# One stage in place of combining, residual, last norm and store, and an earlier split of the last expert's lower weights

## The reference

```python
def expert_block(args):
    idx, w, e = args
    xb = tok_pad[idx]
    hb = jax.nn.silu(xb @ ex_gate[e]) * (xb @ ex_up[e])
    return (hb @ ex_down[e]) * w[:, None]
...
ffn = _hier_moe(_modulate(x, sh2, sc2), ...)
x = _layernorm(ALPHA * x + g2 * ffn, ln2_g[l], ln2_b[l])
```

## Time and profile before

| | us |
|---|---|
| median of three runs | 3562.02 |
| the profiled execution, its own time | 3566.95 |
| span of the profiled execution | 3565.2 |
| from the last expert's result copy (DVE, 3486.77) to the end of the span | 78.4 |
| PE busy, share of the span | 88% |
| DVE busy, share of the span | 56% |
| mean granted TensorE clock | 0.946 |

### The profile page before, as it was taken

One profiled execution on the slowest core, in us unless ns is written; L12 is line 12 of the kernel. 1 busy time (PEld: TensorE's weight loads), 2 busy tenths in 40 slices (PEclk: granted clock), 3 DMA queues, 4 the chain that ended last, 5 costly groups with the idle time before them and its releaser, 6 DMA issues. The chain is left out here.

```text
span 3565.2 us, 53470 instructions
## 1 busy us (share of the span) xinstructions
PE 3146.9 (88%) x21844; PEld 2464.7 (69%) x21844; DVE 2002.8 (56%) x2748; ACT 1284.8 (36%) x1613; POOL 910.2 (26%) x472
## 2 busy tenths in 40 slices
PE   7968999997999978999889998389997869999993
PEld 5446887796777756887678766268885358888882
DVE  3756551301433346553399447775644359998983
ACT  2543322222333333332232212312222247777772
POOL 3013443342222213443312300010100014454530
PEclk9989999999999989999999998699998979999996
DMA  3631222321111111222311100401001149999992
GB/s 137 235 119 71 94 94 83 124 95 71 60 60 60 60 48 71 94 94 84 106 48 60 59 17 1 176 23 50 26 26 75 47 168 360 364 372 367 374 355 100
DMA packets 76463, 439.37 MB, mean 123 GB/s; under 512 B 14832, under 2 KB 17904, under 8 KB 27376
## 3 DMA queue, kind: packets, MB, share of 16 engines
q1 hardware_dynamic: 66768, 427.12, 32.3%
q0 software_dynamic: 9504, 9.47, 0.8%
HBM read 421.85 MB, written 39.85 MB: 130 GB/s over the span
## 5 line engine op out<-in xcount | busy, mean ns | idle before, releaser
L76 POOL TENSOR_TENSOR ring_lo<-ring,unit_hi 128x2048 fp32r<-128x2048 f32 x116 | 536.2, 4624 | 1206.3 <-ACT unit_hi L71 1206.3
L122 PE MATMUL wide<-h_hi,unit_hi 128*128 128x512 f32 x1296 | 519.7, 401 | 99.9 <-DVE h_lo L182 43.5
L124 PE MATMUL wide<-h_hi,ring_lo 128*128 128x512 f32 x1296 | 519.1, 401 | 0.0
L123 PE MATMUL wide<-h_lo,unit_hi 128*128 128x512 f32 x1296 | 518.0, 400 | 0.0
L3013 DVE TENSOR_TENSOR ex_w_lo<-ring,ex_w_hi 128x2048 fp32r<-128x2048 f32 x192 | 437.2, 2287 | 43.5 <-ACT ex_w_hi L2966 41.6
L2966 ACT CAST ex_w_hi<-ring 128x2048 fp32r<-128x2048 f32 x192 | 365.7, 1908 | 103.7 <-DMA ring<-in_weights 91.1
L71 ACT CAST unit_hi<-ring 128x2048 fp32r<-128x2048 f32 x116 | 220.3, 1900 | 459.3 <-PE wide L124 450.7
L122 PEld LDWEIGHTS wide<-h_hi,unit_hi 128*128 128x128 f32 x1296 | 250.9, 194 | 178.6 <-POOL ring_lo L76 70.7
L123 PEld LDWEIGHTS wide<-h_lo,unit_hi 128*128 128x128 f32 x1296 | 247.0, 191 | 53.2 <-issue 0.2
L124 PEld LDWEIGHTS wide<-h_hi,ring_lo 128*128 128x128 f32 x1296 | 246.4, 190 | 52.7
L363 DVE TENSOR_TENSOR ffn_hidden_lo<-ffn_whole,ffn_hidden_hi 128x512 f32 (+1 forms) x44 | 201.5, 4579 | 50.6 <-ACT ffn_hidden_hi L338 50.6
(11 more groups left out here) (528 smaller groups left out, 6205.2 us busy)
## 6 DMA issues: line engine op xcount, KB each, us to landing
ring<-in_weights SPq DMA_DIRECT2D x356, 1024.0 KB
factors<-rp_out SPq DMA_DIRECT2D x8, 1536.0 KB, 5.5
rw_F<-factors SPq DMA_DIRECT2D x12, 1024.0 KB, 5.6
cb_both<-pair_rows_out SPq DMA_DIRECT2D x4, 1024.0 KB, 4.8
x<-in_x SPq DMA_DIRECT2D x1, 2048.0 KB, 7.5
x_kept<-x SPq DMA_DIRECT2D x1, 2048.0 KB, 12.2
x<-x_kept SPq DMA_DIRECT2D x1, 2048.0 KB, 8.9
x_mixing<-x SPq DMA_DIRECT2D x1, 2048.0 KB, 10.7
```

What stands on the lines that cost most here:

```text
L76: pool.tensor_tensor(self.lo[n % RING][:, :], self.ring[n % RING][:, :], self.hi[n % 2][:, :].bitcast(F32), ALU.subtract).then_inc(lo_read ...
L122: pe.matmul(dst, a[0], b[0], start=start, stop=False)
L123: pe.matmul(dst, a[0], b[1], start=False, stop=False)
L124: return pe.matmul(dst, a[1], b[0], start=False, stop=stop)
```

## The change

Two edits. The last expert's two down units are split in step 31, right after its gating product, and no longer at the start of step 32. And the four blocks after the experts become one, `tail_stage`: SP issues all four loads at once, each with a semaphore of its own; ACT scales `x` by ALPHA meanwhile; PE transposes each chunk of features into a PSUM bank of its own; DVE adds gate times that bank to `x` straight from PSUM; PE sums each chunk as it is added; the norm is the class `Norm`, with two buffers for the squares; and each of the 8 chunks is stored (256 KiB each) as soon as it is placed.

```diff
                 def step(e, j2, s):
-                    if s >= 1:
+                    if 1 <= s < EXPERTS:
                         for n in range(2):
                             hi(e, down_at(s - 1, n))
...
                         hi(e, gate_up_at(s + 1, 2))
+                    elif s == EXPERTS - 1:
+                        for n in range(2):
+                            hi(e, down_at(s, n))
...
-                    if s >= 1:
+                    if 1 <= s < EXPERTS:
                         for n in range(2):
                             lo(e, down_at(s - 1, n))
...
                         lo(e, gate_up_at(s + 1, 2))
+                    elif s == EXPERTS - 1:
+                        for n in range(2):
+                            lo(e, down_at(s, n))
...
-def combine_stage(nc, c, route, pair_rows, y):
+def tail_stage(nc, c, route, pair_rows, x, gate, scale, shift, out):
...
+        both, squares, rstd = sb("both", [P, TT, 2, D]), sb("squares", [P, 2, T]), sb("rstd", [P, T])
+        norm = Norm(c, x, x, x, scale, shift, c.bank[0], c.bank[1], squares, rstd[:, :])
...
                 for t in range(TT):
                     sp.dma_start(both[:, t, :, :].rearrange("p n d -> p (n d)"),
-                                 pair_rows[2 * P * t:2 * P * (t + 1), :].rearrange("(p n) d -> p (n d)", n=2)).then_inc(loaded, 16)
-
-                    sp.wait_ge(loaded, 16 * (t + 1))
+                                 pair_rows[2 * P * t:2 * P * (t + 1), :].rearrange("(p n) d -> p (n d)", n=2)).then_inc(loaded[t], 16)
+                for k in range(DC):
+                    sp.wait_ge(norm.placed, k + 1)
+                    sp.dma_start(out[:, k, :], x[:, k, :]).then_inc(stored, 16)
+                sp.wait_ge(stored, 16 * DC)
+
+            @block.scalar
+            def _(act):
+                for m in range(DC):
+                    act.mul(x[:, m, :], x[:, m, :], ALPHA).then_inc(grown, 1)
+                norm.scalar(act)
 
             @block.vector
             def _(dve):
                 for t in range(TT):
-                    dve.wait_ge(loaded, 16 * (t + 1))
+                    dve.wait_ge(loaded[t], 16)
...
-                for t in range(TT):
-                    dve.wait_ge(turned, 2 * t + 2)
-                    dve.tensor_copy(y[:, 4:8, t * P:(t + 1) * P], c.wide[t][:, T:D].rearrange("p (k t) -> p k t", k=4)).then_inc(high_done, 1)
+                for k in range(DC):
+                    dve.wait_ge(turned, k + 1)
+                    dve.wait_ge(grown, k + 1)
+                    dve.scalar_tensor_tensor(out=x[:, k, :], in0=c.bank[k], scalar=gate(k), in1=x[:, k, :], op0=ALU.mult,
+                                             op1=ALU.add).then_inc(added, 1)
+                norm.vector(dve)
 
             @block.tensor
             def _(pe):
                 for t in range(TT):
                     pe.wait_ge(summed, t + 1)
                     for k in range(DC):
-                        mm = pe.transpose(c.wide[t][:, k * P:(k + 1) * P], both[:, t, 0, k * P:(k + 1) * P], c.ident[:, :])
-                        if k % 4 == 3:
+                        mm = pe.transpose(c.bank[k][:, t * P:(t + 1) * P], both[:, t, 0, k * P:(k + 1) * P], c.ident[:, :])
+                        if t == TT - 1:
                             mm.then_inc(turned, 1)
...
+                for k in range(DC):
+                    pe.wait_ge(added, k + 1)
+                    norm.sum_chunk(pe, k)
+                pe.wait_ge(added, 2)
+                norm.sum_squares(pe)
...
-        combine_stage(nc, c, route, pair_rows, dev)
-        last_residual_stage(nc, c, x, dev, at(5))
-        layer_norm_stage(nc, c, x, x, T, col("ln2_g"), col("ln2_b"), "ln2")
...
+        tail_stage(nc, c, route, pair_rows, x, at(5), col("ln2_g"), col("ln2_b"), out)
```

More of the change, by code:

```diff
@@ L3053, in experts_stage, with sb @@
     w.at += ALL
-def combine_stage(nc, c, route, pair_rows, y):
+def tail_stage(nc, c, route, pair_rows, x, gate, scale, shift, out):
     with ExitStack() as ctx:
-        both = ctx.enter_context(nc.sbuf_tensor("cb_both", [P, TT, 2, D], F32))
-        loaded, scaled, summed, turned, low_done, high_done = c.semaphores("cb", ("loaded", "scaled", "summed", "turned", "low_done", "high_done"))
+        def sb(n, shape):
+            return ctx.enter_context(nc.sbuf_tensor(f"tail_{n}", shape, F32))
+        both, squares, rstd = sb("both", [P, TT, 2, D]), sb("squares", [P, 2, T]), sb("rstd", [P, T])
+        norm = Norm(c, x, x, x, scale, shift, c.bank[0], c.bank[1], squares, rstd[:, :])
+        fresh = norm.use(c.semaphores("tail", [f"norm_{n}" for n in Norm.NAMES] + [f"loaded{t}" for t in range(TT)] + [
+            "grown", "scaled", "summed", "turned", "added", "stored"]))
+        loaded, (grown, scaled, summed, turned, added, stored) = fresh[:TT], fresh[TT:]
         with nc.Block() as block:
```

## The result

The changed kernel takes 3543.15 us (median of 6 runs, 3533.86 to 3546.82) against 3567.41 us before (6 runs, 3556.59 to 3572.75): 24.3 us between the medians, a ratio of 0.9928 with a 95% interval of 0.9914 to 0.9941 (21 to 31 us). 27.0 had been forecast, for 3535.0 us. Of the 8.2 us between 3535.0 and 3543.15, 5.4 are the base (the median of before rose from 3562.02 to 3567.41 with three more runs) and 2.7 the gain. The profiled execution of after took 3534.85 us (span 3533.1), that of before 3566.95.

A forecast was written before the change was run, and what follows sets the result against it. PE, busy 88% of the span, bounds most of the kernel; gains lie in the last 100 us. Terms 6.2 + 6.35 + 8.6 + 1.85 + 4.0 = 27.0 us, off 3562.0, give 3535.0 us, range 3525 to 3547.

The forecast's parts named there:

- C: Last load's landing to end of sums over x: 13.0 us instead of 21.6, saving 8.6 us (7.4 to 11.5).
- E: Eight stores at the end: span ends 2.9 us after the last chunk instead of 6.87, saving 4.0 us.
- A: Earlier split before the last down product: 3.2 us less waiting and 3.0 from the kept clock, saving 6.2 us.
- Rival 1: Clock lost after shorter gaps and transposes don't start its rise: 5.3 us less, saving 21.7, 3540.3 us; chance 0.14.
- B: Four tail loads issued at once: last lands 12.9 us after first issue instead of 19.25, saving 6.35 us.
- rival 2: Four tail loads finish together near 12.9 us: 6.2 us less, saving 20.8, 3541.2 us; chance 0.09.
- D: Norm after the sums over x: 20.40 us instead of 22.25, with PE's clock kept, saving 1.85 us.
- Rival 3: Last expert's split comes no earlier because unit 191 lands after 3473: saving 20.8, 3541.2 us; chance 0.05.
- Rival 5: Changed step code makes the experts' loop stall PE each pass: at 1.5 us costs 46.5, giving 3581.5 us; chance 0.03.

The follow-up runs named there:

- e1: Kernel before with only the earlier split of the last two down units, the blocks after the experts unchanged; 3.6 us faster than before (0.9991).
- e5: Changed kernel with the late split and five idle float32 matmuls on PE in the gap before the last down product; 24.7 us under before.
- e6: Changed kernel with PE waiting for all four sums before its first transpose, so 32 run in one piece; 19.8 us faster than before (0.9946).
- e8: Changed kernel with early loads plus idle PE matmuls before the last down product and in the tail; 28.3 us faster than before (0.9924).
- e2: Changed kernel with the split of the last two units put back to the start of step 32; 23.4 us faster than before (0.9938).
- e0: Changed kernel run again without an edit, on the chip of other runs; 26.6 us faster than before (0.9930).
- e7_early_loads: Changed kernel with SP issuing the four loads within the experts' block once the last scatters landed; 28.5 us under before (0.9922).
- e3: Changed kernel with SP waiting for each of the four loads before issuing the next; 15.8 us faster than before (0.9953).
- e4: Changed kernel with one 2 MiB store after the last placed chunk instead of eight of 256 KiB; 24.1 us under before (0.9937).
- e7_again: Repeat of the changed kernel with the four loads issued early from the experts' block; 27.9 us under before (0.9924).

## Why the prediction was right, and where its sizes were off

What each of the five terms removes was right, and the sum, 27.0 us, lies inside the measured 21 to 31. One mechanism inside term C was not: the time that the clock takes to rise. And it was partly luck that the sum came so close, for C and E gave more than forecast, A less on average, and the medians less than the traces. By step, with the traces:

- **A, 6.2 us.** Measured 6.1 (after, e1), and 4.9 to 3.5 where the last unit landed later. Over the eight traces with the early split and no idle work the mean is 5.0. Both halves are shown: the wait (gap 1.60 for the 1.75 worked out) and the clock (e5). Rival 1 was half right: in three of the eight traces the clock was lost after this gap, at 1.3 to 1.6 us, about half of the 3.0 that it was priced at. Its other two parts did not happen: the transposes do start the rise (e6), and "norm" is 20.46 us in every trace with the new tail, so no clock was lost there.
- **B, 6.35 us.** Measured 6.4 (19.25 to 12.84). The four loads landed in order and 2.5 to 3.0 us apart (once 3.8, in e8), not together, so rival 2 falls.
- **C, 8.6 us.** This is the term that was mis-sized: from the last landing to the end of the sums I had 13.0 us, and it was 10.5 and 11.7 in the changed kernel's two traces (11.0 in e2). Saved: 11.2 and 10.0. The prediction let the clock rise 6.0 us after the last group of transposes began, a time read from the kernel before. Both halves failed. With the loads close together the groups follow each other within 0.5 to 1.0 us, and the level rose 6.9 us after the first of the four (after; 3493.91 to 3500.8), 11.1 (e0) and 9.4 (e2); from the last group on it was 3.2 us in e0 and 1.7 in e2, and in after it had risen already. And 6.0 us is no constant: with PE working without a stop the rise came after 6.0 us (the down product and the sums before), 6.2 (the product in e2), 5.0 (the sums in e1), 2.8 (the product in e6), 2.9 (in e7_early_loads) and 3.1 (the transposes in e6). In after, PE was at full before the sums began, and C came close to the end of the range that the prediction gave it for that case (11.5). The prediction's other figure for C, 7.4 if transposes do not start the rise, is off by more: they do (e6).
- **D, 1.85 us.** Measured 1.8: 20.46 for 20.40, in place of 22.25. The table load hid behind the wait for the variance, as said.
- **E, 4.0 us.** Measured 4.4 (6.87 to 2.44); the small backlog that the sum allowed for is not there.

Rival 3 did not happen: unit 191 landed before PE's transposes in every trace, though in the worst cases late enough to cost 1.2 us of wait. Rival 5 did not either, at its size: "experts" is 581.7 to 589.7 us in the ten traces with the changed step code, where it forecast 46.5 us more than the 584.7 of before. Their mean is 586.0, that of the three traces with the old code (before, e2, e5) 583.8; single traces vary by 8 us, so a loss of 2 us is neither shown nor excluded.

In the traces after and e0 give 29.9 and 27.5 us from the last expert on, and the first medians 24.3 with some 5 us of uncertainty from the experts' stage and its start. That is enough to account for the difference, but a small loss in that stage would do it too. What makes the stage vary by 8 us from run to run was not looked into.

One sentence of the text ahead of the prediction is wrong: PE is not busy for at most 12 of any 20 us at the end of the kernel before. From 3526 to 3546 us, over the sums over x and of the squares, it is busy for 17.8 of 20. PE and its clock weigh most there, and terms C and D lie in that stretch.

## What to carry to other kernels

Merge small stages where each ends in a full wait: a load, a sum or a store that can follow the piece before it hides nearly all of its own time, and the gain can be read off as intervals between waits. When an edit is worth less than the spread of the whole, compare the same interval in each run's own trace; here 3 us were visible that the medians could not show. The intervals do not replace the time, though: if the medians keep falling short of them, something outside may have changed. And a wait of PE can have a second price, the lower clock on the work behind it. The same program paid it in some executions and not in others, so look at more than one trace before you count it as won, and don't carry a time to the rise from one place to another.

## What the runs showed of the hardware

- Transposes alone brought TensorE's clock up, 3.1 us after the first of 32 in one piece (e6). In groups of 2.0 us every 4.8 us they didn't (e3); in groups about 2.5 us apart the rise came 4.2 (e7_early_loads) to 11.2 us (e4) after the first began, counting the sums behind them.
- The level falls and rises at varying distances. Before the down product, gaps of 1.6 to 1.8 us did not cost it in four traces, gaps of 2.6 to 2.8 us did in three of four; a gap of 1.36 us between transposes did once. After PE stopped, it fell 2.1 us (e6, before the product) to 5.2 us later (after, behind the product); in e7_again it fell 4.1 us after the stop, when PE had been working again for 1.4 us.
- GpSimd's drain at the end of the experts' block takes 6.56 us in every trace, in after ending 3.7 us past the end of the scatter's data. A semaphore of the scatter let SP go on 3.3 us earlier.
- Four loads of 1 MiB queued together moved 4.2 MB in 12.8 us from issue to use; after the first landing each took 2.5 to 3.0 us (3.8 once), where one alone takes 4.8.
